# Slab splits held behind the first head's softplus remainder, a later output split, and a reordered seventh head in a stick-breaking and differential attention kernel

## The reference, cut to what matters

```
def stick_breaking_layer(x, norm_g, w_in, w_out):
    h = rms_norm(x, norm_g)
    q, k, v, gate = split(h @ w_in, 4)
    z = q.k / sqrt(64)                                   # per head, strictly causal
    log_1m = where(strict, log_sigmoid(-z), 0)
    suffix = reverse_cumsum(log_1m) - log_1m
    a = where(strict, exp(log_sigmoid(z) + suffix), 0)
    return (silu(gate) * (a @ v)) @ w_out

def diff_layer(x, k, v, ...):
    q, gate = split(rms_norm(x, norm_g) @ w_in, 2)
    q = rope(rms_norm(q, q_norm_g))
    p = softmax(causal(q.k / sqrt(64)))                  # two components
    o = rms_norm((p[0] - lam * p[1]) @ v, subln_g) * (1 - lam_init)
    return (silu(gate) * o) @ w_out
```

## Time and profile before

| what | value |
|---|---|
| median of 3 runs | 661.46 us (661.09 to 663.24) |
| the profiled execution's own time | 661.75 us |
| its span, first to last instruction | 660.5 us |
| TensorE busy | 628.2 us, 95% |
| VectorE busy | 443.5 us, 67% |
| ScalarE busy | 336.3 us, 51% |
| GpSimd busy | 352.2 us, 53% |
| mean granted TensorE clock | 0.990 of full |
| chain that ended last | PE 63%, DVE 21%, ACT 6%, issue 5%, POOL 3% |

### The profile page before, as it was taken

The page is one execution under the profiler, slowest core; times in us unless marked ns, Lnnn a source line. Parts: engine busy times, 40 slices in busy tenths (PEclk is TensorE's granted clock), DMA queues, the critical chain, the costliest instruction groups (busy, mean ns, idle before and its releaser), DMA issues.

```text
span 660.5 us, 9992 instructions
## 1 busy us (share of the span) xinstructions
PE 628.2 (95%) x3324; PEld 528.0 (80%) x3324; DVE 443.5 (67%) x701; ACT 336.3 (51%) x728; POOL 352.2 (53%) x339
## 2 busy tenths in 40 slices
PE   5899999999999999989999999999899999969998
PEld 4788778888888888868877888788788888867876
DVE  3484197977969688593336398425979999966531
ACT  5342366674857657574326534323565565545320
POOL 4665595564555645183542455457765557733261
PEclk9999999999999999999999999999899999979999
DMA  7432131212211111022110222232322222121041
GB/s 253 108 112 82 50 110 50 65 48 64 64 48 48 51 61 62 0 82 77 66 64 34 96 96 95 82 106 62 87 65 73 55 79 80 41 72 33 32 160 64
DMA packets 61773, 49.08 MB, mean 74 GB/s; under 512 B 7728, under 2 KB 48816, under 8 KB 61744
## 3 DMA queue, kind: packets, MB, share of 16 engines
q1 hardware_dynamic: 58064, 48.25, 23.7%
q10 hardware_dynamic: 3680, 0.46, 0.5%
HBM read 44.50 MB, written 2.10 MB: 71 GB/s over the span
## 4 chain that ended last, share of the span: by engine, by line
PE 63%; DVE 21%; ACT 6%; issue 5%; POOL 3%; DMA 1%; DVEq 0%; SPq 0%; ACTq 0%; POOLq 0%
PE bank L582 16%; PE bank L583 15%; PE bank L584 15%; PE bank L696 6%; DVE hi L1452 4%; PE bank L710 3%; DVE sp L1446 2%; DVE lo L1457 2%; ACT pr L1289 2%; PE bank L681 2%; POOL w_lo L477 1%; ACT ex L1106 1%; DVE small L1646 1%; DMA xs<-in_x 1%; DVE h_hi L1414 1%
## 5 line engine op out<-in xcount | busy, mean ns | idle before, releaser
L477 POOL TENSOR_TENSOR w_lo<-w_raw,w_hi 128x512 fp32r<-128x512 f32 x100 | 146.1, 1461 | 8.0
L465 POOL TENSOR_TENSOR w_lo<-w_raw,w_hi 128x512 fp32r<-128x512 f32 x60 | 82.2, 1377 | 114.9 <-ACT w_hi L993 114.9
L475 POOL CAST w_hi<-w_raw 128x512 fp32r<-128x512 f32 x100 | 72.4, 724 | 130.0 <-PE bank L584 53.1
L582 PE MATMUL bank<-w_hi,h_hi 128*128 128x512 f32 x320 | 127.9, 400 | 6.9 <-POOL w_lo L477 3.0
L582 PE MATMUL bank<-h_hi,w_hi 128*128 128x512 f32 x320 | 131.0, 409 | 2.6 <-ACT q L1205 2.6
L583 PE MATMUL bank<-h_lo,w_hi 128*128 128x512 f32 x320 | 126.8, 396 | 0.0
L584 PE MATMUL bank<-h_hi,w_lo 128*128 128x512 f32 x320 | 126.8, 396 | 0.0
L584 PE MATMUL bank<-w_hi,h_lo 128*128 128x512 f32 x320 | 125.1, 391 | 0.0
L583 PE MATMUL bank<-w_lo,h_hi 128*128 128x512 f32 x320 | 124.9, 390 | 0.0
L582 PEld LDWEIGHTS bank<-w_hi,h_hi 128*128 128x128 f32 x320 | 60.1, 188 | 21.5 <-POOL w_lo L477 4.3
L582 PEld LDWEIGHTS bank<-h_hi,w_hi 128*128 128x128 f32 x320 | 61.0, 191 | 17.1 <-ACT q L1205 2.5
(11 more groups left out here) (174 smaller groups left out, 1201.5 us busy)
## 6 DMA issues: line engine op xcount, KB each, us to landing
w_raw<-in_a_w_in SPq DMA_DIRECT2D x64, 256.0 KB, 2.8
w_raw<-in_w_kv SPq DMA_DIRECT2D x32, 256.0 KB, 3.1
w_raw<-in_b_w_in SPq DMA_DIRECT2D x32, 256.0 KB, 2.8
w_raw<-in_a_w_out SPq DMA_DIRECT2D x16, 256.0 KB, 2.6
w_raw<-in_b_w_out SPq DMA_DIRECT2D x16, 256.0 KB, 3.0
xs<-in_x SPq DMA_DIRECT2D x4, 512.0 KB, 5.2
qrot<-qs SPq DMA_DIRECT2D x32, 64.0 KB, 2.0
out_x<-xs SPq DMA_DIRECT2D x8, 256.0 KB, 2.7
```

The lines of the kernel that those rows point to most:

```text
L465: nc.gpsimd.tensor_tensor(w_lo[s][:, :], w_raw[s][:, :], w_hi[s][:, :].bitcast(F32), ALU.subtract).then_inc(s_w, 1)
L475: nc.gpsimd.tensor_copy(w_hi[s][:, :], w_raw[s][:, :]).then_inc(s_whi, 1)
L477: nc.gpsimd.tensor_tensor(w_lo[s][:, :], w_raw[s][:, :], w_hi[s][:, :].bitcast(F32), ALU.subtract).then_inc(s_w, 1)
L582: pe.matmul(o, ahi, bhi, start=start, stop=False, skip_group_check=True)
```

## The change

It has five parts.

- GpSimd, pairs 1 to 6: after the values' split it waits until the three `lo` pieces of head 0 of this round are written, and only then splits slabs.
- GpSimd, pair 6: the first four slabs of the output projection are split in front of the last pair's values instead of behind them.
- VectorE, first layer: `keep_output` of a pair is done in the next pair's round, behind head 1's softplus and in front of `gate_log`; that of the last pair stays at its end.
- Head 0 of the second layer: ScalarE copies q's third projection in front of the last group of exponentials instead of behind it.
- Head 6 of the second layer: TensorE's `sums` go from in front of the second gate's projection to its middle, in front of the turned weights; ScalarE squares the output right behind the gate's copy and abs, in front of `q_round`, and does the gate's exp and log behind `q_round`; VectorE does `gate_silu` in front of q's addition.

```diff
@@ GpSimd
         with pool.Fori(1, KT - 2) as i:
             st.enter(i, 1, 1)
             values_a(i)
+            pool.wait_ge(s_sl, i * 6 + 3)
             for j in range(6):
                 split(G_BODY + 6 + j, i, 6)
             st.leave(KT - 3)
         values_a(KT - 2)
+        pool.wait_ge(s_sl, (KT - 2) * 6 + 3)
         split(G_GLAST)
         split(G_GLAST + 1)
+        for g in range(G_OUT, G_OUT + 4):
+            split(g)
         values_a(KT - 1)
-        for g in range(G_OUT, N_A):
+        for g in range(G_OUT + 4, N_A):
             split(g)
@@ TensorE, head 6
         attend_before(h, 2)
-        sums(h + 1, h - 1)
+
+        def sum_and_turn_last():
+            sums(h + 1, h - 1)
+            turn_probs(h)
+
         pe.wait_ge(s_gc, h + KT + 1)
         pe.wait_ge(s_ga, h + KT + 1)
-        project(H_GATES + 2, h1_hi, h1_lo, bank[6][:, :], between=lambda: turn_probs(h))
+        project(H_GATES + 2, h1_hi, h1_lo, bank[6][:, :], between=sum_and_turn_last)
@@ ScalarE
-        def gate_parts(h, used):
+        def gate_copies(h, used):
 
             act.wait_ge(s_si, h + KT)
             gate_copy(used)
             gate_abs_a(h + (KT + 1))
+
+        def gate_parts(h, used):
+
+            gate_copies(h, used)
             gate_log(h + (KT + 1))
...
                 if b == 1 and gate is not None:
                     gate_exp(h + KT)
-            if q_used is not None:
+                if b == 1 and first:
+                    q_copy(h + 3, q_used)
+            if q_used is not None and not first:
                 q_copy(h + 3, q_used)
             if later is not None and h == KT - 2:
-                gate_parts(h, later)
+                gate_copies(h, later)
+                output_square(h - 1)
             if q_next:
                 act.wait_ge(s_z, h * 6 + 54)
                 q_round(h + 1)
-            if not first:
+            if later is not None and h == KT - 2:
+                gate_log(h + (KT + 1))
+            elif not first:
                 output_square(h - 1)
@@ VectorE
             TTN(og[:, :], osum[:, :], silu[:, :], ALU.mult).then_inc(s_og, 1)
-            keep_output(p, p + 1)
...
             soft_hi(5)
             soft_lo(5)
+            if not first:
+                keep_output(p - 1, p)
             gate_log(p + 1)
...
         finish(KT - 1, bank[0], bank[3])
+        keep_output(KT - 1, KT)
...
             combine((3, 2), 2, 4)
+            if silu_first:
+                gate_silu(h + KT)
             if q_next:
                 q_add(h + 2)
-            if gate:
+            if gate and not silu_first:
                 gate_silu(h + KT)
...
-        head(KT - 2, 2, q_after=False)
+        head(KT - 2, 2, q_after=False, silu_first=True)
```

More of the change, by code:

```diff
@@ L1439, in finish, with pair @@
             TTN(og[:, :], osum[:, :], silu[:, :], ALU.mult).then_inc(s_og, 1)
-            keep_output(p, p + 1)
-        def pair(p, last=False):
+        def pair(p, first=False, last=False):
             def soft(m):
@@ L1544, in _ @@
             V.tensor_copy(v32[:, n % TT, cols(HALF, HALF)], bank[n % 6][:, :]).then_inc(s_vkd, 1)
-        pair(0)
+        pair(0, first=True)
         with dve.Fori(1, KT - 1) as i:
@@ L1634, in o_times_gate, with head @@
                 op1=ALU.mult).then_inc(s_ot, 1)
-        def head(h, n_before, q_next=True, q_after=True, gate=True):
+        def head(h, n_before, q_next=True, q_after=True, gate=True, silu_first=False):
             def biases(v, b):
```

## The result

The changed kernel takes 651.38 us (median of 4 runs, 650.17 to 652.19); the kernel before took 662.35 us on the same chip (4 runs, 661.09 to 663.55). The ratio is 0.9833, 95% interval 0.9805 to 0.9861: 1.7% faster. The forecast was 649.2 us with a range of 645.5 to 654.5. Of all the executions reported here one, of e5, ran at a mean granted clock of 0.847 and took 710.44 us; it is left out of e5's numbers.

The account below looks back on a forecast made before the run. TensorE is busy nearly throughout, so time can come only from its idle stretches or its clock; 3.4 + 3.0 + 0.2 + 5.7 = 12.3 us off the median 661.46 gives 649.2 us, range 645.5 to 654.5.

Parts of the forecast that it names:

- The waits in the rounds: Pairs 1 to 6, first suffix sum: TensorE's wait for head 0's `lo` goes, 0.56 us a round, 3.4 us in all.
- What is late next: Pairs 1 to 6, VectorE's head 1 beside the delayed splits: takes 7.1 us, ends 1.5 us before needed, no new wait.
- rival 1: Rounds: the collision moves to head 1, losing 5.3 us instead of gaining 3.4, 657.9 us in full; chance 0.10.
- the bad bound: Rounds: all three splits delay head 1 in full, a 1.4 us wait, net loss 0.9 us a round, 5.3 in all.
- `keep_output` and the slabs' lateness at nothing: Rounds: `keep_output` behind head 1 costs 0 with 1 us of cover; delayed slabs, needed over 15 us later, cost 0.
- Last pair: Between 278 and 300 us: TensorE's three waits for GpSimd go, 3.0 us gained (bounds 2.3 and 3.5).
- Head 0: Second layer: the wait for q shrinks 1.1 us, but TensorE then waits for VectorE's combine; 0.2 us gained.
- Head 6: Second layer: the idle stretch before the sums and the half clock behind it go; 5.7 us gained (bounds 4.6 and 6.5).
- the counted half collision: Head 6: one more `w_lo` blocking the next gate's log or silu costs 1.3 us, counted half the time.
- rival 2: Head 6's wait moves to the early tile and lowers the clock there: gain 2.9 instead of 5.7, 652.0 us; chance 0.08.
- The sum: Whole kernel: the terms 3.4, 3.0, 0.2 and 5.7 us make 12.3 us saved.

Follow-up runs that it names:

- e5: The changed kernel with `keep_output` back at the end of its own pair, in front of head 0's softplus of the next round; 652.62 us, ratio 0.9854.
- e1: The changed kernel without GpSimd's two waits for head 0's remainder before its slab splits; 656.5 us, ratio 0.9895.
- e9: The changed kernel with GpSimd's slab splits in pairs 1 to 6 held until the remainders of both heads are written; 651.77 us, ratio 0.9826.
- e2: The changed kernel with the first four output projection slabs split behind the last pair's values again; 654.63 us, ratio 0.9889.
- e3: The changed kernel with q's third copy behind the last exponentials of head 0 (second layer) again; 650.97 us, ratio 0.9819.
- e4: The changed kernel with all edits of head 6 (TensorE, ScalarE, VectorE) undone; 657.82 us, ratio 0.9933.
- e7: The changed kernel with GpSimd's last two early output slabs and head 6's values held until head 7's gate is multiplied out, slabs first; 651.33 us, ratio 0.9829.
- e6: The changed kernel with GpSimd's next slab splits in head 0 of the second layer held until the weights are combined; 649.65 us, ratio 0.9808.
- e8: The changed kernel with pair 0's slab splits, from the fifth on, held until head 0's remainder is written; 651.18 us, ratio 0.9836.

## Why the prediction was right, step by step

**The waits in the rounds: right, a little small.** Forecast 0.56 us a round, measured 0.70. A matmul that starts behind a wait takes 0.50 us instead of 0.40 (the earlier trace rows against the row of the changed kernel above); with these 0.1 the sum is 0.66. e1 shows the cause by giving the 0.70 back. The blocked times were priced right: the copies came out at 0.42 and 0.29 us (forecast 0.43 and 0.28), the `lo` at 0.68, and a head without collisions at 4.3 us in e9 (forecast 4.3).

**What is late next: right in its answer, optimistic in its size.** Head 1 was to take 7.1 us and end at 152.6; it took 7.6. The changed kernel's pair 2 begins 1.1 us later than before's (first scores at 138.16 against 137.02), so 152.6 corresponds to 153.7, and the end at 154.22 is 0.5 us late. TensorE wanted it at 154.88, 0.3 earlier than the 154.1 + 1.1 that I had reckoned. Of 1.5 us of cover 0.66 were left; rival 1 missed by no more than that. The mechanism is in the rows above: behind each of GpSimd's operations one of VectorE's gets through, and the next is blocked again (`lo` 1.18, 1.44 and 1.47 us). The Trainium skill's rule ("SBUF — State Buffer", section "SBUF: two separate sides") that the one that starts first holds the port for its whole instruction fits these rows. e9 beside the changed kernel gives its price for a head, 4.3 against 7.6 us. One sum of mine was off: the bad bound is 1.4 - 0.56 = 0.84 us a round, 5.0 in all and not 5.3; nothing hangs on it.

**`keep_output` and the slabs' lateness at nothing: shown for the rounds** by e5 and e9. In e9 the splits start still later, and a round keeps its 27.59 us. In the last pair `keep_output` was not nothing, as e2 shows.

**Last pair: 3.0 forecast, 3.1 measured, but my reason explains only part.** I put all of it on the four splits; e2 gives back 2.0. The other 1.1 us I had put at nothing: by the traces of the kernel before and e2 it is `keep_output`, which no longer slows the first output splits. So the size of this term came out right in part by luck. The 0.4 us that are left of the wait for `lo` were foreseen (up to 0.6).

**Head 0: the term with the wrong sign.** Forecast 0.2 us gained, measured 1.24 lost. The first half held: TensorE waits 1.0 us less for q and then waits for the combine, which ends 12.6 us into the head (before 12.75). The turns begin 0.4 us earlier, as priced. But in the kernel before the 3.4 us of low clock lay in front of the turns, where TensorE would have waited anyway; now they lie behind, where nothing hides them, and half of 3.4 us is 1.7: 1.7 - 0.4 = 1.3. I had priced just this ("up to 1.7 us are lost") and left it out of the value I took, although a wait was certain to stand in front of the new place. The edit to q brought nothing (e3): without it head 0 is shorter and the next two heads longer by the same 1.7 us.

**Head 6: right.** Forecast 5.7 us, measured 5.5; e4 gives back 5.1. In detail: the projection starts 9.19 us into the head (forecast 583.7 - 574.5 = 9.2). The last `at_lo` ends at 18.4 instead of 18.1, the early tile starts at 22.75 instead of 21.8 without and 22.5 with the counted half collision. Two operations on this way were held by GpSimd, 1.1 us by the split of head 6's values and 1.0 us by a slab split:

```profile
585.67 1.29 POOL L501 TENSOR_TENSOR vb_lo<-v,vb_hi 128x512 fp32r<-128x512 f32 x1 [0.18 <-POOL vb_hi L499]
```

```profile
585.56 0.17 DVE L1361 SCALAR_TENSOR_TENSOR small<-small 128x12 f32<-128x12 f32 x1
585.76 1.23 DVE L1362 SCALAR_TENSOR_TENSOR small<-small 128x12 f32<-128x12 f32 x1
```

and `silu` at 1.68 us, shown under e7 with its 0.69 for comparison. The collision that I had counted half the time came in full. The wait before the early tile was 1.8 us (forecast 1.4 without collision, under 2), and the clock held in the changed kernel; rival 2 named this place rightly, and in e6 and e8 the low clock did come there.

**The sum.** By stages 4.18 + 3.11 - 1.24 + 5.47 = 11.5 us against 12.3 forecast. The rounds brought 0.8 us more than forecast and head 0 1.4 less, so two misses partly cancel; that the total is so near is in part luck. The profiled executions differ by 9.6, since the later start (+1.8) stands against it; the medians by 11.0.

## What to carry to other kernels

Holding GpSimd back by a semaphore doesn't make its work shorter; it chooses which of VectorE's operations pay for it, so look for a stretch whose results are wanted late (here head 1, whose 3.3 us of blocking cost nothing), and hold GpSimd until it begins. What is held falls on something later: each of the three further holds gave part of its gain back in the next stages (0.4 to 0.7 us in heads 1 to 5, 0.7 behind head 6, 1.5 in pair 1). A wait that is shortened and reappears behind the next operation may cost more than it did, because a low clock that follows it then lies on the path, as in head 0. Where whole runs scatter by 2 us and stages repeat within 0.2, compare stages.

## What was unexpected in the hardware

- GpSimd's hold isn't in proportion to VectorE's operation. A `small` operation of 12 columns took 1.23 us beside a split, a like one 0.17 alone (head 6's rows above), so a chain of small ones on the critical path suffers most for its work.
- The same idle length has two outcomes for the clock. The wait in front of the early tile was 1.84 us in e3, e6 and e8 alike: it was followed by 3.4 us at the lower level in e6 and e8, and by none in e3. In head 0 a wait of 2.1 us was followed by 3.4 us of it in the changed kernel and 6.8 in e1, one of 1.8 us in e7 by 3.4, and a first wait of 2.1 us in e3 by none. Such a stretch costs 1.6 us (the rest in e6 and e8 against the changed kernel), which is most of what single edits of this size bring or cost; what decides between the outcomes no run here shows. The Trainium skill ("TensorE: Matmul & The Clock Gate", section "HAM oscillation — how this bites in real kernels") has idle stretches of a few microseconds between matmuls send the array to half rate; in this kernel waits of 1.8 to 2.1 us were followed by it too. The prediction's reading, that a wait of 1.4 us keeps the clock and one of 3 us would not, left these in between unpriced.
